# A high weight part times both activation parts in one 512-column matmul, with the halves summed behind it

## What is computed

```python
def swiglu(x, w_in, w_out):
    g, u = jnp.split(x @ w_in, 2, axis=-1)
    return (jax.nn.silu(g) * u) @ w_out
...
for i in range(DEPTH):                       # DEPTH = 2
    h = h + 0.5 * swiglu(rms_norm(h, ffn1_norm[i]), ffn1_w_in[i], ffn1_w_out[i])
...
    h = h + m
    h = h + 0.5 * swiglu(rms_norm(h, ffn2_norm[i]), ffn2_w_in[i], ffn2_w_out[i])
```

## Time and profile before

| | |
|---|---|
| time, median of 3 runs | 1570.32 us (1567.24 to 1570.74) |
| span of the profiled execution, first to last instruction | 1566.5 us |
| TensorE clock granted, mean over the span | 0.986 |
| PE busy, PEld busy | 1522.4 us (97%), 1463.1 us (93%) |
| DVE, ACT, POOL busy | 1051.3 us (67%), 768.2 us (49%), 289.2 us (18%) |
| DMA | 153 GB/s mean, q1 holds 48.5% of 16 engines |

### The profile page before, as it was taken

The page is one execution under the profiler, slowest core; times in us unless marked ns, Lnnn a source line. Parts: engine busy times, 40 slices in busy tenths (PEclk is TensorE's granted clock), DMA queues, the critical chain, the costliest instruction groups (busy, mean ns, idle before and its releaser), DMA issues.

```text
span 1566.5 us, 31432 instructions
## 1 busy us (share of the span) xinstructions
PE 1522.4 (97%) x11949; PEld 1463.1 (93%) x11949; DVE 1051.3 (67%) x1997; ACT 768.2 (49%) x1274; POOL 289.2 (18%) x350
## 2 busy tenths in 40 slices
PE   7999998999999999999999998999999999999998
PEld 6999998999999999999999997888898999888898
DVE  6666579766656665567766556896678678765783
ACT  5544457554535454454545434446544453564442
POOL 4111112211111111131311023432100124321000
PEclk9999999999999999999999998999999999999999
DMA  6556753465555655554665553433333543333333
GB/s 202 188 180 197 242 164 122 150 199 179 177 188 173 190 180 182 181 177 134 189 187 182 175 180 94 139 106 95 96 95 108 176 143 115 95 95 109 98 120 120
DMA packets 245275, 239.65 MB, mean 153 GB/s; under 512 B 15160, under 2 KB 244392, under 8 KB 245048
## 3 DMA queue, kind: packets, MB, share of 16 engines
q1 hardware_dynamic: 245176, 238.29, 48.5%
HBM read 237.21 MB, written 1.05 MB: 152 GB/s over the span
## 4 chain that ended last, share of the span: by engine, by line
PE 85%; DVE 10%; ACT 2%; issue 2%; POOL 1%; DMA 0%; SPq 0%; DVEq 0%; ACTq 0%; POOLq 0%
PE bank L526 25%; PE bank L528 25%; PE bank L527 25%; DVE w_lo L1439 2%; PE bank L842 1%; PE bank L801 1%; PE bank L780 1%; PE bank L779 1%; ACT w_hi L925 1%; PE bank L760 1%; DVE work L1592 1%; DVE work L1479 1%; PE bank L847 1%; PE bank L856 0%; PE bank L812 0%
## 5 line engine op out<-in xcount | busy, mean ns | idle before, releaser
L1439 DVE TENSOR_TENSOR w_lo<-raw,w_hi 128x1024 fp32r<-128x1024 f32 (+1 forms) x456 | 556.6, 1229 | 319.0 <-ACT w_hi L925 318.8
L526 PE MATMUL bank<-x_hi,w_hi 128*128 128x256 f32 (+1 forms) x2480 | 722.7, 291 | 6.7 <-DVE x_lo L1452 5.2
L528 PE MATMUL bank<-x_hi,w_lo 128*128 128x256 f32 (+1 forms) x2480 | 709.5, 286 | 0.0
L527 PE MATMUL bank<-x_lo,w_hi 128*128 128x256 f32 (+1 forms) x2480 | 708.7, 286 | 0.0
L925 ACT CAST w_hi<-raw 128x1024 fp32r<-128x1024 f32 (+1 forms) x456 | 465.3, 1029 | 275.9 <-PE bank L528 261.2
L526 PEld LDWEIGHTS bank<-x_hi,w_hi 128*128 128x128 f32 x2480 | 478.2, 193 | 15.8 <-issue 10.9
L527 PEld LDWEIGHTS bank<-x_lo,w_hi 128*128 128x128 f32 x2480 | 478.7, 193 | 0.8
L528 PEld LDWEIGHTS bank<-x_hi,w_lo 128*128 128x128 f32 x2480 | 478.1, 193 | 0.0
L526 PE MATMUL bank<-y_hi,w_hi 128*128 128x256 f32 (+1 forms) x1088 | 311.0, 286 | 8.1 <-DVE y_lo L1450 8.1
L528 PE MATMUL bank<-y_hi,w_lo 128*128 128x256 f32 (+1 forms) x1088 | 310.1, 285 | 0.0
L527 PE MATMUL bank<-y_lo,w_hi 128*128 128x256 f32 (+1 forms) x1088 | 310.0, 285 | 0.0
(11 more groups left out here) (259 smaller groups left out, 1244.5 us busy)
## 6 DMA issues: line engine op xcount, KB each, us to landing
raw<-in_ffn_w_in_dram SPq DMA_DIRECT2D x176, 512.0 KB, 3.6
raw<-in_w_in_dram SPq DMA_DIRECT2D x100, 512.0 KB, 3.4
raw<-in_ffn_w_out_dram SPq DMA_DIRECT2D x64, 512.0 KB, 3.8
raw<-in_w_out_dram SPq DMA_DIRECT2D x32, 512.0 KB, 3.5
raw<-in_ffn_w_out_dram SPq DMA_DIRECT2D x32, 384.0 KB, 3.0
raw<-in_rec_w_in_dram SPq DMA_DIRECT2D x16, 512.0 KB, 3.3
raw<-in_sg_w_in_dram SPq DMA_DIRECT2D x16, 512.0 KB, 3.3
raw<-in_rec_w_out_dram SPq DMA_DIRECT2D x8, 512.0 KB, 3.4
```

Source lines behind the costliest of these rows:

```text
L526: mm(acc, wh, xh, start=first and j == 0, stop=False)
L527: mm(acc, wh, xl, start=False, stop=False)
L528: i_ = mm(acc, wl, xh, start=False, stop=last and j == n - 1)
L1439: TT(w_lo[:, s, 0:n, :], raw[:, s, 0:n, :], w_hi[:, s, 0:n, :].bitcast(fp32), SUB).then_inc(lo_made, 1)
```

## The change

For the pairs in the set `HALVES` (all four in phases, all six out phases of the first block, and `proj1`) a triple becomes two matmuls. One has 512 columns: the high weight part times the high and the low activations side by side, which go to the two halves of a bank. The other has 256 columns: the low weight part times the high activations, which is added into the second half. For this, `x_hi` and `x_lo` become two planes of one tensor `x_s`, and `y_hi` and `y_lo` of `y_s`. The tile is then the sum of two halves of a bank.

In the in phases DVE sums the halves with a `tensor_reduce` (`whole`) into `ffn_t`, for gate and up tiles alike. The multiplication by `rstd` and the product of gate and up, which DVE did while it read PSUM, become GpSimd instructions (`gate_normed`, `gated_up`). In the out phases DVE adds the two halves to `h` one after the other.

```diff
+HALVES = set()
+for _n in ("in01", "out01", "rec_out", "in02", "out02", "in11", "out11", "sg_out", "in12", "out12", f"proj{DEPTH - 1}"):
+    _, _b, _k = PHASES[_n]
+    HALVES.update(range(_b, _b + _k))
...
+                        if pair in HALVES:
+                            both = bank[T % 4][:, :].rearrange("p (h n) -> p h n", h=2)
+                            small = bank[T % 4][:, SEQ:2 * SEQ]
+                            if opens:
+                                mm(both, wh, xs[:, :, cols], start=True, stop=False)
+                                mm(small, wl, xs[:, 0, cols], start=False, stop=False)
+                            else:
+                                mm(small, wl, xs[:, 0, cols], start=False, stop=False)
+                                i_ = mm(both, wh, xs[:, :, cols], start=False, stop=closes)
...
             def gate_turn(ub, i, f, first=None):
...
                 for m in range(2):
-                    act.wait_ge(tile_read, 2 * pb + m + 1 + o4)
+                    act.wait_ge(gate_normed, 22 * f + m + 1 + 2 * i)
                     activation(ffn_s[:, m, :], ffn_t[:, m, :], ACT.Silu).then_inc(silu_done, 1)
                 for U in (ub + 2, ub + 3):
                     split_w(U + LEAD, o)
                 for m in range(2):
-                    act.wait_ge(tile_read, 2 * pb + 2 + m + 1 + o4)
+                    act.wait_ge(gated_up, 22 * f + m + 1 + 2 * i)
...
                 def turn(i):
+                    for m in range(2):
+                        pool.wait_ge(tile_read, 2 * pb + m + 1 + 4 * i)
+                        TT(ffn_t[:, m, :], ffn_t[:, m, :], rstd[:, META:L], MUL).then_inc(gate_normed, 1)
                     for m in range(2):
                         pool.wait_ge(silu_done, 22 * f + m + 1 + 2 * i)
                         TT(ffn_r[:, m, :], ffn_s[:, m, :], rstd[:, META:L], MUL).then_inc(gate_scaled, 1)
+                    for m in range(2):
+                        pool.wait_ge(tile_read, 2 * pb + 2 + m + 1 + 4 * i)
+                        pool.wait_ge(gate_scaled, 22 * f + m + 1 + 2 * i)
+                        pool.wait_ge(act_ready, count + m - 1 + 2 * i)
+                        TT(ffn_h[:, m, :], ffn_t[:, m, :], ffn_r[:, m, :], MUL).then_inc(gated_up, 1)
...
+            def whole(dst, pr, m):
+                halves = bank[(2 * pr + m) % 4][:, :].rearrange("p (h n) -> p n h", h=2)
+                return V.tensor_reduce(dst, halves, mybir.AxisListType.X, ADD)
...
                 for m in range(2):
-                    scaled(pb, m, ffn_t[:, m, :], SEQ, META, o)
+                    wait_tile(pb, m, o)
+                    if f or not isinstance(i, int):
+                        dve.wait_ge(gated_up, 22 * f + m - 1 + 2 * i)
+                    whole(ffn_t[:, m, :], pb, m).then_inc(tile_read, 1)
                 for U in (ub + 2, ub + 3):
                     split_w(U + LEAD, o)
                 for m in range(2):
                     wait_tile(pb + 1, m, o)
-                    dve.wait_ge(gate_scaled, 22 * f + m + 1 + 2 * i)
-                    TT(ffn_h[:, m, :], tile(pb + 1, m, SEQ), ffn_r[:, m, :], MUL).then_inc(tile_read, 1)
+                    dve.wait_ge(silu_done, 22 * f + m + 1 + 2 * i)
+                    whole(ffn_t[:, m, :], pb + 1, m).then_inc(tile_read, 1)
...
-                        STT(out=h[:, c, T0:L], in0=tile(pb + p, m, N), scalar=half, in1=h[:, c, T0:L], op0=MUL,
-                            op1=ADD).then_inc(tile_read, 1)
+                        i_ = STT(out=h[:, c, T0:L], in0=tile(pb + p, m, N), scalar=half, in1=h[:, c, T0:L], op0=MUL, op1=ADD)
+                        if pb + p in HALVES:
+                            link(i_)
+                            i_ = STT(out=h[:, c, T0:L], in0=low(pb + p, m), scalar=half, in1=h[:, c, T0:L], op0=MUL, op1=ADD)
+                        i_.then_inc(tile_read, 1)
```

More of the change, by code:

```diff
@@ L196, in build_stack @@
         h = sb("h", [P, NC8, L])
-        x_hi = sb("x_hi", [P, NC8 * L], fp32r)
-        x_lo = sb("x_lo", [P, NC8 * L], fp32r)
-        y_hi = sb("y_hi", [P, NF * SEQ], fp32r)
-        y_lo = sb("y_lo", [P, NF * SEQ], fp32r)
+        x_s = sb("x_s", [P, 2, NC8 * L], fp32r)
+        y_s = sb("y_s", [P, 2, NF * SEQ], fp32r)
+        x_hi, x_lo = x_s[:, 0, :], x_s[:, 1, :]
+        y_hi, y_lo = y_s[:, 0, :], y_s[:, 1, :]
         con = sb("con", [P, CONST_ALL])
@@ L293, in build_stack @@
         act_new = sem("act_new")
-        silu_done, gate_scaled = sem("silu_done"), sem("gate_scaled")
+        gate_normed, silu_done, gate_scaled, gated_up = (
+            sem(n) for n in ("gate_normed", "silu_done", "gate_scaled", "gated_up"))
         par_loaded, con_loaded, x_loaded, blk_loaded, sg_loaded, first_par = (
@@ L506, in unit @@
                      mid=None):
-                hi, lo = xs
                 pe.wait_ge(lo_made, U + 1 + off)
@@ L521, in unit @@
                         wh, wl = (t[:, s, j, m * P:(m + 1) * P] for t in (w_hi, w_lo))
-                        if N == SEQ and wide_x:
-                            xh, xl = (t[:, k * L + META:(k + 1) * L] for t in (hi, lo))
-                        else:
-                            xh, xl = xview(hi, k, N), xview(lo, k, N)
-                        mm(acc, wh, xh, start=first and j == 0, stop=False)
-                        mm(acc, wh, xl, start=False, stop=False)
-                        i_ = mm(acc, wl, xh, start=False, stop=last and j == n - 1)
+                        cols = slice(k * L + META, (k + 1) * L) if N == SEQ and wide_x else slice(k * N, (k + 1) * N)
+                        opens, closes = first and j == 0, last and j == n - 1
+                        if pair in HALVES:
[7 more added lines that the diff above has]
+                                i_ = mm(both, wh, xs[:, :, cols], start=False, stop=closes)
+                        else:
+                            acc = bank[T % 4][:, 0:N]
+                            mm(acc, wh, xs[:, 0, cols], start=opens, stop=False)
+                            mm(acc, wh, xs[:, 1, cols], start=False, stop=False)
+                            i_ = mm(acc, wl, xs[:, 0, cols], start=False, stop=closes)
                     if last and m == 0 and tiles == 2:
@@ L545, in pair @@
                         after(j)
-            xs, ys = (x_hi, x_lo), (y_hi, y_lo)
+            xs, ys = x_s, y_s
             def norm_sum(n, T0):
@@ L912, in _ @@
         def _(act):
+            F_OF = {"in01": 0, "in02": 1, "in11": 2, "in12": 3}
             activation = nc.scalar.activation
@@ L950, in root, with gate_turn @@
                 activation(rms[:, T0:L], bank[4][:, T0:L], ACT.Sqrt, scale=1.0 / D, bias=epsc[:, 0:1]).then_inc(rms_done, 1)
-            def gate_turn(pb, ub, i, first=None):
-                o4, o = 4 * i, (4 * i if not isinstance(i, int) else 4 * i)
+            def gate_turn(ub, i, f, first=None):
+                o = 4 * i
                 for U in (ub, ub + 1):
@@ L973, in in_phase @@
             def in_phase(name, n):
-                ub, pb, _ = PHASES[name]
-                gate_turn(pb, ub, 0, first=n)
+                ub, f = PHASES[name][0], F_OF[name]
+                gate_turn(ub, 0, f, first=n)
                 with act.Fori(1, FF // CU) as i:
-                    gate_turn(pb, ub, i)
+                    gate_turn(ub, i, f)
             def out_phase(name, g, N=SEQ, T0=META, before=None, sq=True):
@@ L1333, in _ @@
             nc.gpsimd.memset(rec_p[:, :, 0:3], 0.0).then_inc(zero_set, 1)
-            gate_scale(0)
+            gate_scale(0, "in01", SPLITS["y_out01"])
             h_squares(1, "out01", META)
@@ L1346, in _ @@
             h_squares(2, "rec_out", META)
-            gate_scale(1)
+            gate_scale(1, "in02", SPLITS["y_out02"])
             h_squares(3, "out02", META)
-            gate_scale(2)
+            gate_scale(2, "in11", SPLITS["y_out11"])
             h_squares(4, "out11", META)
@@ L1363, in _ @@
             nc.gpsimd.tensor_scalar(neg_tail[:, :], sink_tail[:, :], -1.0, None, MUL).then_inc(cleared, 1)
-            gate_scale(3)
+            gate_scale(3, "in12", SPLITS["y_out12"])
             h_squares(6, "out12", META)
```

6 lines of the change are left out of this document (4 added, 2 removed).

## The result

| | before | changed |
|---|---|---|
| median of the runs, us | 1568.78 (1566.03 to 1570.74, 4 runs) | 1598.23 (1597.74 to 1599.03, 4 runs) |
| ratio, 95% interval | 1 | 1.0198 [1.0185, 1.0211] |
| profiled span, us | 1566.5 | 1596.2 |

What follows compares the result with a forecast made beforehand. PE bounds the kernel now; after the change the DVE, ACT and POOL loop binds the in phases. In phases +20.7, out phases -22.5, mixer waits +9.1, small terms +1.0: +8.3 on span 1566.5, plus 3.8, gives 1579 us; range 1557 to 1609.

Steps and rivals of the forecast that it cites:

- I take 0.216, nearer to the row of long passes: PE's price in us for a 512-column matmul, between bounds 0.214 and 0.227; it makes a triple 24 ns cheaper.
- the wide matmul keeps the 13 ns: Rival, chance 0.13: the overhead stays, the out phases give 12.5 us instead of 23.0, and the time is 1589.
- stock of split units: Splits running three units ahead in the in phases; claimed used up in the first turn, then PE waits twice per turn.
- early waits: Behind each in phase, the next phase's second unit waits 0.6 us and its fourth 0.7.
- late chunks and the last tile: Small additions: +0.5 us for chunks that come just late, +0.5 for the last tile's second pass before the output.
- The turn: In phases: the closed loop of ACT, DVE and POOL takes 12.10 us per turn, longer than PE's 10.75.
- The step from pair to pair in `sg_out`: From one pair's first `h` to the next: 5.63 us becomes 6.55, over PE's 5.38.
- The price of the second pass over `h` behind the mixers: After `rec_out` and `sg_out`, PE waits 4.6 us in the second unit of `in02` and of `in12`: +9.1 us.
- the sign named for the loop: In the changed profile's in phases, PE idles before D and B, released by DVE `w_lo`, 1.35 us per turn.
- 3.8 us between span and time: The median of the runs lies 3.8 us above the span, so a span of 1574.8 gives 1578.6.
- neither cheap nor dear: Two rivals on the in phases' reduce: 0.42 us, priced by output, 1557 (chance 0.17); 1.22 us, twice the price, 1656 (0.07).
- Contention: Rival, chance 0.07: one POOL product per turn at 1.48 us in the in phases' loop adds 30 us, 1608.

Runs made afterwards that it cites:

- pe_forms: A kernel of its own, computing none of the reference: streams of 32 float32r matmuls per width, other engines quiet, then DVE and ACT busy; 512 columns cost 228 ns.
- outs_only: The kernel before, with the wide matmul only in the four long out phases and `proj1`: 1561.66 us, 0.9975 of before.
- combined: The changed kernel with gate products on DVE, ACT's early `w_hi` of B, later decay constants, and `rec_out` and `sg_out` as before: 1553.14 us, 0.9916 of before.
- narrow_halves: The changed kernel with all wide matmuls of a tile but the first and last made as two narrow ones: 1596.71 us, 1.0194 of before.
- late_decay: The changed kernel with the recurrent mixer's decay constants made behind the second pair of `out01`: 1589.91 us, 1.0161 of before.

## Why the prediction was wrong

**The failed step.** "I take 0.216, nearer to the row of long passes": the wide matmul costs 0.228 among its like, 0.231 beside narrow ones, and 0.236 in the long out phases of the changed kernel (mean distance of starts), where the narrow one costs 0.117. A block saves 7 ns instead of 24, 960 x 17 = 16.3 us of the 17.8 missed in the outs. Of these 17 ns `pe_forms` shows 12, the kept fixed part; the other 5 appear in the kernel alone. The traces rule some causes out. A second piece doesn't cost them in `pe_forms`. In `out02` of `outs_only` the wide matmul takes 236 ns whether POOL works beside it or not (19 and 143 of them), and whether the DMA engines are over 80% or under 10% busy (76 and 51). And in `proj1` of `outs_only`, of `combined` and of the changed kernel it takes 231, as in `pe_forms`. `proj1` reads its activations at other offsets, 272 columns apart and not 256; no run tried that, and the cause of the 5 ns is open. I had the price from a float32 matmul of 256 columns, whose two passes together take 0.44 us. That row shows another kind of matmul, and says nothing on whether float32r keeps a fixed part; the rival *the wide matmul keeps the 13 ns* was right and underpriced.

**A step that was missing.** The stock of split units had a second use. I counted 1.3 us of early waits behind every in phase, and left out that in `out01` 4.5 us of other work stand ahead of the first splits. `out01` took 6.8 us more than the 62.13 of `outs_only`, 5.5 beyond the 1.3 allowed: 4.9 of waits for `w_lo` (0.73 and 4.13), and about 1.9 behind them, mostly while PE ran at half its clock. Behind the other three in phases the early waits were only about 0.6 each (`out02` 62.72, `out11` 62.80 against the 62.13 of `outs_only`), 2 us better. 16.3 + 5.5 - 2.0 = 19.8 is 2.0 more than the outs' 17.8; the forecast had 1.0 for late chunks and the last tile, which may not have been needed, and the rest is not assigned.

**What was right.** The turn: 12.10 forecast, 12.06 measured, with its terms: the reduce 0.69 (683 ns), and from the first gate reduce to the second Silu 2.29 (356.89 to 359.12, 2.23). `narrow_halves` shows that PE doesn't count in it. The handover from `w_hi` to `w_lo` and the two `w_lo` came as in the walk too (359.44 to 360.51 to 362.79). The step from pair to pair in `sg_out`, 6.55 forecast, is 776.89 - 770.35 = 6.54 here:

```profile
770.35 0.41 DVE L1558 SCALAR_TENSOR_TENSOR h<-bank,h 128x256 f32<-128x256 f32 x1
770.80 0.42 DVE L1561 SCALAR_TENSOR_TENSOR h<-bank,h 128x256 f32<-128x256 f32 x1
...
776.89 0.41 DVE L1558 SCALAR_TENSOR_TENSOR h<-bank,h 128x256 f32<-128x256 f32 x1
```

**Right by luck, or only in part.** The price of the second pass over `h` behind the mixers was forecast as 9.1 us and found as 9.2 when it was taken out. But PE's waits for `x_s` in `in02` and `in12` sum to 5.2 us, in four waits of 0.9 to 1.9, and not to two of 4.6. In both phases a stretch at half clock follows, which the forecast had nothing of. `late_decay` shows its price: it has the same waits in `in12` (3.1 us in both kernels), no such stretch, and takes 135.13 there against 136.61. And the sign named for the loop, PE idle for 1.35 us per turn, was off: it is about 0.7, as PE's own turn is some 11.2 us (32 x 0.35) and not 10.75. The turn of the loop, 12.06, doesn't change by that.

**A small slip in the sum.** The forecast put 3.8 us between span and time, from a span and a median of different executions. In one and the same execution it is 1.8 before (1566.9 and 1568.66) and 2.1 in the changed kernel (1596.2 and 1598.26), so the sum gives 1577 and not 1579.

**The other rivals.** The reduce is priced by its input (683 ns; `tensor_reduce` at 1x, as the Trainium skill has it under VectorE: DVE Perf Modes, The perf-mode tier table), and its two halves 1 KB apart cost nothing, so it was neither cheap nor dear. Contention didn't enter the changed kernel's loop: POOL's products took 738. It stood 0.03 us away (POOL's scalings end at 359.04 + 1.44 = 360.48, the `w_lo` starts at 360.51; the prediction had 0.05), and came with the first edit that moved a `w_lo`.

**What stays open.** 3.1 us arose in parts whose code is the same. That is little: the spans of the kernel before alone lie between 1562.2 and 1568.4 us over its executions. In these parts a phase takes 1.5 to 1.6 us more where a stretch at half clock falls into it: `mg1` took 38.97 us with one and 37.41 without. The changed kernel has 13 such stretches, 55.8 us in all, against 9 of 44.6 before and 8 of 39.5 in `combined`. Three of them follow new waits of PE: at 163.7, behind the wait of 4.13 us; at 313.9, in the second of two waits for `x_s` (0.91 and 1.23); and at 788.3, behind two more. Before, the clock was at its upper level (2.4 GHz) all through `out01`, `in02` and `in12`. All five kernels in which PE waits for 4 us or more at the start of `out01` have the first of these stretches, and the other four, like the kernel before, have none there. But a wait doesn't always bring one: `late_decay` has the waits in `in12` and no stretch. Two of these stretches of the changed kernel (busy us and count of PE, PEld, DVE, ACT and POOL, then the granted clock, where 0.50 is 1.2 GHz):

```profile
163.70:167.10 3.40, 3.40 (x13) 2.81 (x12) 2.09 (x3) 0.00 (x0) 0.00 (x0) 0.50 0.76 216
313.90:317.30 3.40, 3.00 (x10) 2.61 (x11) 2.64 (x3) 3.37 (x5) 0.00 (x0) 0.50 0.12 40
```

Why it fell more often in the later stages too was not settled.

## What to carry to other kernels

A matmul's fixed part is measured for the very type and the very mix, before a merge of matmuls is counted on: here the block gave 7 ns of the 24 counted on. When a step is put into a ring of engines, walk the whole ring, and then ask what the stock that it eats up had been hiding elsewhere. Two shortenings of a ring can be worth little each and much together, when each alone only lets the next constraint, here contention on GpSimd, take its place.
